# Hybrid diffusion backbone on one core: conditioning weights spread over three stages instead of two

## What is computed

```python
for i in range(DEPTH):
    mx = jnp.split(cond_x @ ada_w[i] + ada_b[i], 6, axis=-1)
    mc = jnp.split(cond_c @ ada_w[i] + ada_b[i], 6, axis=-1)
    hx = modulate(rms_norm(x, g[0]), mx[0], mx[1])      # shift, scale of the mixer
    ox, oc = mixer(hx, hc, ...)
    x = x + mx[2] * rms_norm(ox, g[1])                  # gate of the mixer
    x = x + mx[5] * rms_norm(sq_relu_mlp(modulate(rms_norm(x, g[2]), mx[3], mx[4]), ...), g[3])
...
def mamba_out(y, xs, z, d_skip, norm_g):
    y = (y + xs * d_skip[:, None]).reshape(bsz, L, D_INNER)
    return rms_norm(y * jax.nn.silu(z), norm_g)         # the gated norm
```

## Time and profile before

| | |
|---|---|
| median of 3 runs | 3930.78 us (3930.62 to 3931.12) |
| profiled execution, its own time | 3941.41 us |
| span of that profile | 3939.6 us |
| TensorE busy | 3535.0 us, 90% |
| VectorE, ScalarE, GpSimd busy | 48%, 33%, 17% |
| DMA | 410 MB, mean 104 GB/s |
| opening | 0 to 87.9 us of the span |
| first projection stage | 87.9 to 251.8 us |
| gated norm | 2610.8 to 2631.7 us |

### The profile page before, as it was taken

One profiled execution on the slowest core, in us unless ns is written; L12 is line 12 of the kernel. 1 busy time (PEld: TensorE's weight loads), 2 busy tenths in 40 slices (PEclk: granted clock), 3 DMA queues, 4 the chain that ended last, 5 costly groups with the idle time before them and its releaser, 6 DMA issues. The chain is left out here.

```text
span 3939.6 us, 40323 instructions
## 1 busy us (share of the span) xinstructions
PE 3535.0 (90%) x15656; PEld 2500.0 (63%) x15656; DVE 1888.4 (48%) x2385; ACT 1295.8 (33%) x2063; POOL 678.8 (17%) x418
## 2 busy tenths in 40 slices
PE   5986799999889999999997898757898789999997
PEld 2654244455678888888885686532344568888886
DVE  3221644433356544645764332865155456445544
ACT  4322334444544323423542132220110243233222
POOL 0000267766321101100301001310000121001001
PEclk7998889999999999999998998876999899999999
DMA  7743623311244323333652210020320233333333
GB/s 289 272 155 106 158 54 62 90 48 47 75 141 136 113 95 105 131 98 100 200 159 84 80 38 13 1 87 16 124 96 27 86 124 123 96 97 112 128 95 105
DMA packets 141393, 410.03 MB, mean 104 GB/s; under 512 B 24717, under 2 KB 41645, under 8 KB 137044
## 3 DMA queue, kind: packets, MB, share of 16 engines
q1 hardware_dynamic: 141204, 407.46, 32.2%
HBM read 346.11 MB, written 61.21 MB: 103 GB/s over the span
## 5 line engine op out<-in xcount | busy, mean ns | idle before, releaser
L1486 DVE TENSOR_TENSOR w_low<-w_raw,w_high 128x1024 fp32r<-128x1024 f32 x360 | 450.2, 1251 | 239.3 <-ACT w_high L1401 239.1
L1401 ACT ACTIVATE w_high<-w_raw 128x1024 fp32r<-128x1024 f32 x360 | 379.3, 1054 | 501.6 <-PE psum L1377 454.3
L1360 PE MATMUL psum<-h_high,w_high 128*128 128x512 f32 (+1 forms) x1280 | 476.9, 373 | 9.5 <-DVE w_low L1486 9.3
L1377 PE MATMUL psum<-hid_high,w_high 128*128 128x512 f32 (+1 forms) x1280 | 473.6, 370 | 8.2 <-DVE w_low L1486 8.1
L1360 PE MATMUL psum<-h_low,w_high 128*128 128x512 f32 (+1 forms) x1280 | 471.5, 368 | 0.0
L1360 PE MATMUL psum<-h_high,w_low 128*128 128x512 f32 (+1 forms) x1280 | 471.5, 368 | 0.0
L1377 PE MATMUL psum<-hid_low,w_high 128*128 128x512 f32 (+1 forms) x1280 | 470.7, 368 | 0.0
L1377 PE MATMUL psum<-hid_high,w_low 128*128 128x512 f32 (+1 forms) x1280 | 470.7, 368 | 0.0
L1569 POOL TENSOR_TENSOR squares_then_rstd_of_out<-squares_then_rstd_of_out,square_out 128x512 f32<-128x512 f32 (+1 forms) x70 | 96.6, 1380 | 1322.1 <-ACT square_out L1416 1321.9
L1148 POOL TENSOR_TENSOR probs_added<-probs_added,probs_turned 128x1024 f32<-128x1024 f32 x128 | 304.7, 2380 | 71.5 <-ACT probs_turned L1077 67.0
L1116 DVE TENSOR_REDUCE row_max<-psum 128x1 f32<-128x1280 f32 x128 | 190.3, 1491 | 248.1 <-PE psum L1025 147.3
(11 more groups left out here) (393 smaller groups left out, 5487.5 us busy)
## 6 DMA issues: line engine op xcount, KB each, us to landing
w_raw<-in_ff_w_dram SPq DMA_DIRECT2D x320, 512.0 KB
ada_ring<-in_ada_w_dram SPq DMA_DIRECT2D x24, 2048.0 KB, 9.0
w_raw<-in_w_out_dram SPq DMA_DIRECT2D x40, 512.0 KB
stream_in<-scratch_x SPq DMA_DIRECT2D x32, 256.0 KB, 4.2
scratch_spectra<-spectrum_out SPq DMA_DIRECT2D x32, 256.0 KB, 2.0
filter_ring<-scratch_spectra SPq DMA_DIRECT2D x16, 512.0 KB, 4.2
w_raw<-in_w_hy_dram SPq DMA_DIRECT2D x12, 512.0 KB
scratch_hyena<-hy_conv SPq DMA_DIRECT2D x12, 512.0 KB
```

The costliest lines, as they stand in the source:

```text
L1360: mm = pe.matmul(bank[:, 0:n], x[:, i % 2, k, :], y[:, k, a:a + n], start=(k == 0 and m == 0), stop=(k == KT - 1 and m == 2))
L1377: mm = pe.matmul(bank[:, 0:n], x[:, i % 2, 2 * k + half, :], y[:, k, 0:n], start=(k == 0 and m == 0), stop=(k == HT - 1 and m == 2))
L1401: act.activation(w_hi[:, i % 2], raw[:, i % 2], ACT.Copy).then_inc(w_rounded, 1)
L1486: dve.tensor_tensor(w_lo[:, i % 2], raw[:, i % 2], w_hi[:, i % 2], ALU.subtract).then_inc(w_split, 1)
```

## The change

The 24 pieces are shared out anew. `opening` keeps its four needed pieces and gives up the other five. The first projection stage computes 17 instead of 15: pieces 4 to 11 of layer 0 and 0 to 8 of layer 1. The last three, pieces 9 to 11 of layer 1, move to `gate_norm`, which gets a `Modulation` of its own with two PSUM banks. They are needed first in the MLP of layer 1, behind it. In the first projection stage the order of SyncE's first loads changes, and TensorE's wait for the four tables moves behind the first product.

```diff
-ADA_FIRST = [(0, piece) for piece in (2, 3, 0, 1, 4, 5, 6, 7, 8)]
-ADA_LATER = [(0, piece) for piece in (9, 10, 11)] + [(1, piece) for piece in range(ADA_PIECES)]
+ADA_FIRST = [(0, piece) for piece in (2, 3, 0, 1)]
+ADA_LATER = [(0, piece) for piece in range(4, ADA_PIECES)] + [(1, piece) for piece in range(9)]
+ADA_LAST = [(1, piece) for piece in (9, 10, 11)]
...
-        AFTER = {8: 4, 11: 5, 14: 6, 17: 7, 20: 8}
...
-                for i in range(NEEDED, A):
-                    ada.multiply(pe, i)
-                    ada.turn(pe, i)
...
-                        if q + 1 in AFTER:
-                            ada.copy(act, AFTER[q + 1])
...
-                            if q - LAG + 1 in AFTER:
-                                ada.bias(dve, AFTER[q - LAG + 1])
...
-                for t in range(2):
-                    ring.load(sp, t, d["w_qk"][t])
-                for dst, src in ((cos, "cos_a"), (sin, "sin_a"), (by_head, "by_head"), (swap, "swap_a")):
+                ring.load(sp, 0, d["w_qk"][0])
+                ada.load_selector(sp)
+                for dst, src in ((by_head, "by_head"), (swap, "swap_a"), (cos, "cos_a"), (sin, "sin_a")):
                     sp.dma_start(dst[:], d[src]).then_inc(tabs_in, 16)
-                ada.load_selector(sp)
+                ring.load(sp, 1, d["w_qk"][1])
...
-                pe.wait_ge(tabs_in, 64)
                 for step in range(U + 2):
+                    if step == 1:
+                        pe.wait_ge(tabs_in, 64)
...
                     ada.turn(pe, step - 1)
                     ada.multiply(pe, step)
+                    if step == U + 1:
+                        ada.turn(pe, step)
...
-def gate_norm(nc, g, xbc, gate, y, out):
+def gate_norm(nc, g, d, xbc, gate, y, out):
...
+        ada = Modulation(nc, g, d, mem, sems[7:], ADA_LAST, (6, 7))
+        A = len(ADA_LAST)
...
+            @block.sync
+            def _(sp):
+                ada.load_selector(sp)
+                for i in range(A):
+                    ada.load(sp, i)
+
             @block.vector
...
+                ada.bias(dve, 0)
                 dve.wait_ge(rstd, 1)
                 for t in range(T):
...
+                for i in range(1, A):
+                    ada.bias(dve, i)
...
                     act.activation(sq[:, t % 2, :], y[:, t, :], ACT.Square).then_inc(squared, 1)
+                ada.copy(act, 0)
                 act.wait_ge(square_used, T)
...
+                for i in range(1, A):
+                    ada.copy(act, i)
...
                     mm.then_inc(square_used, 1)
+                    if t == T - 2:
+                        ada.multiply(pe, 0)
+                ada.turn(pe, 0)
+                for i in range(1, A):
+                    ada.multiply(pe, i)
+                    ada.turn(pe, i)
```

More of the change, by code:

```diff
@@ L189, in opening @@
         ada = Modulation(nc, g, d, mem, sems[15:], ADA_FIRST, (6, 7))
-        A = len(ADA_FIRST)
         x = tile(nc, mem, "x", [P, KT, TOK])
@@ L212, in _ @@
                 load_x(2)
-                for i in range(NEEDED, A):
-                    ada.load(sp, i)
             @block.tensor
@@ L1975, in _ @@
                 y_read(dve, len(ys) - 1)
-def gate_norm(nc, g, xbc, gate, y, out):
+def gate_norm(nc, g, d, xbc, gate, y, out):
     T = 4
-    with stage(nc, "skipped gated squared square_used logged rstd normed") as (mem, (skipped, gated, squared, square_used, logged, rstd, normed)):
+    names = "skipped gated squared square_used logged rstd normed ada_in0 ada_in1 ada_in2 sel_in made copied turned biased folded"
+    with stage(nc, names) as (mem, sems):
+        skipped, gated, squared, square_used, logged, rstd, normed = sems[:7]
+        ada = Modulation(nc, g, d, mem, sems[7:], ADA_LAST, (6, 7))
+        A = len(ADA_LAST)
         sq = tile(nc, mem, "norm_sq", [P, 2, LAT])
@@ L2652, in layer_1 @@
             scan_states(nc, g, d, xbc, gate, dt, adt, ssd)
-        gate_norm(nc, g, xbc, gate, y, y)
+        gate_norm(nc, g, d, xbc, gate, y, y)
         store(nc, y, sc.y)
```

## The result

| | median us | lowest to highest | runs |
|---|---|---|---|
| before | 3930.95 | 3930.16 to 3936.47 | 8 |
| after | 3943.26 | 3937.97 to 3946.22 | 8 |

The ratio is 1.0026 [1.0015, 1.0037]: the change makes the kernel slower by 5.9 to 14.5 us, with 10.2 us as the likeliest (0.0026 x 3930.95). The ratio goes by all runs; the two medians alone lie 12.3 us apart. Both lie above the +4.3 us of the forecast. The first median lies outside its range, the second inside it.

What follows compares the result with a forecast made beforehand. Each stage was read by its own chain: VectorE late in the opening, TensorE in the projection except its ends, VectorE's chain in the gated norm. -7.7 - 2.6 + 11.9 + 2.7 = +4.3 us gave 3935.1 us, range 3928.5 to 3940.5.

Steps and rivals of the forecast that it cites:

- Opening, -7.7: End of the opening: five bias instructions, a fold and their waits leave VectorE's chain, -7.7 us.
- Start, -2.6: Start of the first projection stage: TensorE's first product waits for the weight tile alone, -2.6 us.
- Tail, +11.9: End of the first projection stage: pieces 15 and 16 delay the last store, +11.9 us, bounds +7.8 and +13.9.
- rival 2: Cold throughout: both pieces at the projection's end at half clock (+13.2), sum +5.6 us, 3936.4; chance 0.14.
- Gated norm, +2.7: Gated norm: its three added pieces delay the norm and end the stage later, +2.7 us, bounds +1.2 and +5.3.
- Rival 3: Gated norm's loads share the DMA engines, so its first piece lands late; sum +10.9 us, 3941.7; chance 0.06.
- The clock, 1 us to either side: Rise of TensorE's clock at the projection's start: another phase could be kinder or worse by 1 us, added to both bounds.
- Rivals 1 and 4: 1: projection's end +8.9 or less, sum -0.2 us, chance 0.17; 4: its two pieces hidden, sum -9.1, chance 0.05.

Runs made afterwards that it cites:

- after again: The changed kernel, unaltered, timed in a second series of 11 runs against the kernel before: 3937.67 us, ratio 1.0022.
- after without its pieces: The changed kernel with pieces 15 and 16 of the first projection stage left out, their results zero: 3927.12 us, ratio 0.9990 against before.
- The part alone: The kernel before with only the new order of SyncE's first projection-stage loads and the moved wait for the tables: 3929.71 us, ratio 0.9999.
- the two kernels with the start alone: The kernel before with new load order and moved table wait (3929.71 us, 0.9999), and with the moved wait alone (3931.96 us, 1.0001).

## Why the prediction was wrong

The forecast had the places of the gains and costs right. One step had its mechanism wrong: the start of the projection stage. The tail and the clock's spread were mis-sized, and no single step makes the whole miss. By the timed kernels, -7.1 (opening), 0 (start), +12.6 (tail, as after again less after without its pieces) and +3.9 (gated norm) make +9.4 us, against +10.2 and +8.6 measured. Each of the four is good to 3.5 or 5 us only, and with the other figure for the gated norm, 7.9, they make +13.4: that +9.4 comes so close is partly luck.

- *Opening, -7.7.* Right. The mean over nine profiles with four pieces is 81.3 us, over five with nine pieces 88.2: -6.9; timed -7.1.
- *Start, -2.6.* This step failed: "The bytes ahead of it are unchanged", so the ring's first piece would land at the same distance. The bytes were the same and the landing was 2.3 us later (12.4 instead of 10.1 us; 1.2 us in the mean of seven profiles against seven), because their order had changed. The forecast had seen that only 1.1 us of cover was left. In the profile of after 1.5 us of the gain is left at the first `multiply` (15.68 instead of 17.18 behind the stage's first DMA), 1.0 of that goes into its slower run, and at the end of the last product nothing is left. The same holds in the one other profile in which the first `multiply` ran slow (2.94 us). Over all seven profiles with the new order the last product ends 142.7 us behind the stage's first DMA, over four with before's stage 144.1, over three with the moved wait and before's order 141.4: a gain of 1.4 us in place of 2.6, where 2.7 was to be had. The part alone timed at nothing.
- *Tail, +11.9.* Right in place, and near in size: from the end of the last product to the last low part three profiles have 9.2 to 10.6 us more than before, and the pieces timed at 12.6. The forecast named piece 16's load as the last input; it was the `bias` of piece 15, one step earlier in the same ring of waits. And it took piece 15 at the full clock. In the profile of after both pieces ran at half, in the second profile the first alone. The Trainium skill (TensorE: Matmul & The Clock Gate, Part 1) has the slow clock as the default, and for piece 15, which waited for its load, both traces agree with it (3.64 us behind waits of 2.49 and 3.44). That is rival 2, whose sum of +5.6 was still too low. For piece 16 the two traces part: behind the same wait of 1.74 us it took 3.57 us in one and 1.93 in the other.
- *Gated norm, +2.7.* Right in the profile: +3.1 and +3.0 in the stage. The time gives 3.9 where the pieces are added and 7.9 where they are left out, and does not settle it. Rival 3 is refuted by a first `multiply` that waited for nothing.
- *The clock, 1 us to either side.* This is the term that made the range too narrow. I read the clock's phase at one place and called it 1 us. Two profiles of before differ by 6.4 us, two of after by 12.5 (3944.55, 3932.07), and two medians of after by 5.6 (3943.26, 3937.67). The 19 runs of after have a mean of 3940.1, just inside the range's edge of 3940.5; of the eight that were measured first, six lay above it. No run shows why the first series lies higher than the second.

Two slips in the forecast's working changed little. Its upper bound takes 13.2 us for the tail where its own text has 13.9, which would put the edge at 3940.7. And the ring's second piece lands at 106.3, not 106.8, by the earlier trace rows.

Rivals 1 and 4 fell with the tail: it cost more than 8.9 us in each of the three profiles, and nothing of it was hidden.

**What stays open.** The three stages, each as a mean over its profiles, give -6.9, +10.2 (174.1 for the three with after's stage, 163.9 with before's) and +3.1: +6.4 us. Timed it is 8.8 (3940.1 less 3931.3). The missing 2.4 us are in no stage that I could find: the stretch between the projection stage and the gated norm takes 2348 to 2359 us in the profiles, in no order that follows the kernels, and one profile each cannot resolve them. It is equally open why the start's gain, 1.1 and 3.0 us in the stages of the two kernels with the start alone, does not show in the timings, whose intervals reach to -3.9 and -3.1 us.

## What to carry to other kernels

Work that is added behind the last product of a stage can cost its full chain, loads included: ask what stands behind it in each engine's order, and put it behind the last units' own chain if it must be there. When loads change places in a queue, equal bytes ahead are no proof of an equal landing, and a cover of 1 us is none. And profile the unchanged kernel twice before a forecast of a few microseconds: what its two profiles differ by shows how far a single one can mislead, and the range must allow for it.

## What was unexpected of the hardware

The ring's delay at the start has a mark in the DMA view. Mean busy tenths of the DMA engines and GB/s in 40 slices of 0.4 us from 82 us on, in after:

```profile
DMA  0007489979985989999999989979979979989989
GB/s 0 0 0 101 131 303 364 356 202 205 169 186 154 354 329 354 379 392 402 374 410 463 541 357 617 435 334 526 445 324 526 445 324 526 405 364 526 405 364 526
```

And in before, from 87.5 us on, in slices of 0.35 us:

```profile
DMA  0000949999999999999998996998959899795989
GB/s 0 0 0 0 140 140 363 281 351 421 386 445 442 421 439 424 410 395 439 439 424 345 358 708 237 515 421 374 562 234 515 374 562 421 328 562 234 515 375 562
```

In after the engines move 154 to 205 GB/s for 2 us (slices nine to thirteen) with a busy share of 0.5 to 0.9; in before, with the same tables behind two tiles, the seven slices behind the first of 363 have 281 to 445. At about 350 GB/s the 2 us at half the rate are about 1 us of bytes, so this is part of the 2.3 us and not all of it; SyncE's three ring issues also took 0.53 to 1.11 us each, 0.43 to 0.46 before. The dip goes with the order: in the same view (40 slices of 0.4 us, from 0.44 us ahead of the stage's first DMA) the lowest of slices nine to thirteen is 68 to 156 GB/s in all seven profiles with the new order, and at least 253 in the seven with before's. Why the engines are slower there was not tried.

The other surprise is the clock between 514 and 522 us: one program, one input, and a granted clock of 0.50 in one execution and 1.00 in another.
